# Moving filter-tap sums on GpSimd and the K0 butterfly on VectorE in a Hyena long convolution

## The chip, the cores and the metric

One Trainium2 chip, one core of it. The metric is the device time of the whole program in microseconds, as the median of the runs. The engines are TensorE (PE, with its weight loads as PEld), VectorE (DVE), ScalarE (ACT), GpSimd (POOL) and SyncE (SP), which issues DMAs.

## The reference

The kernel computes one encoder layer for two sequences, a prompt of 1024 tokens and a sample of 512, at a width of 1024: dilated window attention, a bidirectional Hyena branch with two long convolutions one after the other, gates, an output projection and RMS norms. The change lies in the Hyena branch:

```
def _long_conv(z, h_fwd, h_bwd, skip):
    kcirc = jnp.concatenate([h_fwd, jnp.zeros((1, c), jnp.float32), h_bwd[:0:-1]], axis=0)
    spec = jnp.fft.rfft(zf, n=2 * length, axis=1) * jnp.fft.rfft(kcirc, axis=0)[None]
    y = jnp.fft.irfft(spec, n=2 * length, axis=1)[:, :length]
    return y + zf * skip.astype(jnp.float32)
...
    zz = hx1.astype(f32) * _long_conv(hv, filt[:, 0, 0], filt[:, 0, 1], skip[0])
    zz = hx2.astype(f32) * _long_conv(zz, filt[:, 1, 0], filt[:, 1, 1], skip[1])
```

## The kernel before

**Items.** The convolutions run between about 1250 and 2060 us of the span, in 12 items. Items 0 to 7 are long: 256 channels of the prompt at convolution order 0 or 1. Items 8 to 11 are wide: 512 channels of the sample. `wide(i)` tells them apart. Every engine has its own program and passes through the items in order; semaphores hold them together. There are no automatic schedules here; the order on each engine is the order of the code.

**What an item needs.** For each item the filter taps are made on the chip: TensorE makes 8 tiles of taps for forward and backward filters, in four pairs (`gen_pair`, L1263), VectorE multiplies each by its decay (`filt`, L1858, which reads PSUM) into the buffer `hs`, and GpSimd forms the sum and the difference of the forward and backward half of a tile (`sums`, L995 and L996, in `tge`). In long items only tiles 0 to 3 have such sums. The even butterfly (`even_butterfly`, L1893 to L1900, on `tge`) prepares slab K0 of the filter, the odd butterfly (`butterfly_shifted`, L1913 to L1926, on `hs`) the second slab, and the time butterfly (L1893 to L1900 again, on the transposed signal `tz`) the signal's. These are SBUF to SBUF, on VectorE. Two slabs of memory serve for all three in turn, so that a time butterfly overwrites the slab that K0's transforms read and waits for them.

**What a period on VectorE looks like.** `product(i)` goes over four frequency pairs p. For each, it does two filter tiles of the next item (L1858), then the product of signal and filter spectra: two instructions for the real part of the signal (L1964, from PSUM), two for the imaginary part, and one addition in SBUF (L1974). For p = 3, when the next item is long, the even butterfly of the next item comes in front of the filter tiles. Behind the four pairs come the odd and the time butterfly of the next item, then `recombine` twice (L2043 to L2063), which finishes the inverse transform and multiplies with the gate.

**GpSimd beside it.** For each pair it does `sums` of tiles 2p and 2p + 1 of the next item (nothing for tiles above 3 in a long item), then `combine_long`: L1005 adds the two products of the real part, once they are done; L1009 and L1010 add the imaginary parts, once L1974 has run. The event of L1010 (`f_y`) releases the inverse transform of the pair on TensorE and the reuse of the product buffers. A `sums` waits for its filter tile (`f_gen_used`) and, through `f_bf`, for the odd butterfly of the item before.

**TensorE.** `signal_dft` weaves the filter's transforms (K, L1268), the generation of filter pairs (L1263) and the signal's transforms (Z, L1268, one real and one imaginary bank a pair); then the signal of the next item is turned (`to_time`, L1342), inverses 0 and 1 (L1324), the K0 transforms of the next item (L1268, 36 matmuls), which wait for the even butterfly, and inverses 2 and 3. The next item's K transforms wait for the odd butterfly, its Z for the time butterfly. ScalarE copies the results out of PSUM.

**SP.** `load_filter` loads the decay table of the item after (`c_dec`) once the last filter tile of the item in front has been multiplied.

Of the kernel before, what the change touches and what calls it, by code (L numbers as in the profile page):

```python
# [241 lines left out]
def build(nc, ins, cst, y_p, y_s):  # L242
# [7 lines left out]
    with ExitStack() as ctx:  # L250
# [231 lines left out]
        NI = len(ITEMS)  # L482
# [4 lines left out]
        def wide(i):  # L487

            return ITEMS[i][0] == 1

        def chans(i):

            s, q, o = ITEMS[i]
            n = 4 if s else 2
            return n * q, n
# [5 lines left out]
        def zc_of(i):  # L501
            return planes(zc[ITEMS[i][1] % 2], i)
# [16 lines left out]
        def gen_tile(i, j):  # L519

            m, h = j // 2, j % 2
            return (2 * (m % 2) + h, m // 2) if wide(i) else (j, 0)
# [22 lines left out]
        def kernel_units(p):  # L545

            return [K0_UNITS + p, K0_UNITS + 5 + p] + ([K0_UNITS + 4] if p == 0 else [])
# [45 lines left out]
        def wait_free(eng, u):  # L593
            eng.wait_ge(bank_free[u[0]], u[1] + 1)
# [125 lines left out]
        def ot_count(n):  # L720

            return n // 3 + 1
# [16 lines left out]
        def w_allmax(pool, b):  # L739
            pool.wait_ge(S["w_amax"], b + 1)  # L740
            if b >= 3:
                pool.wait_ge(S["w_scale"], b - 2)
            pool.partition_all_reduce(amax_all[b % 3], amax[b % 3], P, bass.bass_isa.ReduceOp.max).then_inc(S["w_all"], 1)  # L743
# [173 lines left out]
        def _(pool):  # L917
# [66 lines left out]
            def sums(i, j):  # L984

                if not wide(i) and j >= 4:
                    return
                t, x = gen_tile(i, j)
                h = hs[:, j % 4 if wide(i) else t, :]
                pool.wait_ge(S["f_gen_used"], GEN0[i] + j + 1)  # L990
                if i >= 1:
                    pool.wait_ge(S["f_bf"], 3 * i - 1)
                c = slice(FQ * x, FQ * x + FQ)
                ge, go = (tge[:, t, c], tgo[:, t, c]) if wide(i) else (tge[:, t, 0:FQ], tge[:, t, FQ:2 * FQ])
                nc.gpsimd.tensor_tensor(ge, h[:, 0:FQ], h[:, FQ:2 * FQ], ALU.add)  # L995
                nc.gpsimd.tensor_tensor(go, h[:, 0:FQ], h[:, FQ:2 * FQ], ALU.subtract).then_inc(S["f_ge"], 1)  # L996

            def combine_long(i, p):

                g = PR0[i] + p  # L1000
                pr, pi = pq[p % 2], pq[2 + p % 2]
                y = yf[:, 2 * p:2 * p + 2, :].rearrange("p b (a c) -> p b a c", a=2)
                part_ = pi[:, 0:4 * FQ].rearrange("p (b a c) -> p b a c", b=2, a=2)
                wait_free(pool, uz[i][2 * p])
                nc.gpsimd.tensor_tensor(yf[:, 2 * p:2 * p + 2, :].rearrange("p b c -> p (b c)"), pr[:, 0:4 * FQ], pr[:, 4 * FQ:8 * FQ],  # L1005
                                        ALU.add).then_inc(S["f_r"], 1)
                pool.wait_ge(S["f_r"], g + 1)
                pool.wait_ge(S["f_im"], g + 1)
                nc.gpsimd.tensor_tensor(y[:, :, 0, :], y[:, :, 0, :], part_[:, :, 1, :], ALU.subtract)  # L1009
                nc.gpsimd.tensor_tensor(y[:, :, 1, :], y[:, :, 1, :], part_[:, :, 0, :], ALU.add).then_inc(S["f_y"], 1)  # L1010

            def combine_wide(i, n):

                a = pq[n % 2]
                if n % 2 == 0:
                    pool.wait_ge(S["f_pq"], 4 * (i - WIDE0) + n // 2 + 1)
                else:
                    wait_free(pool, uz[i][n])
                nc.gpsimd.tensor_tensor(yf[:, n, 0:FQ], a[:, 0:FQ], a[:, 3 * FQ:4 * FQ], ALU.subtract)
                nc.gpsimd.tensor_tensor(yf[:, n, FQ:2 * FQ], a[:, FQ:2 * FQ], a[:, 2 * FQ:3 * FQ], ALU.add  # L1020
                                        ).then_inc(S["f_y"], 1)

            def load_og(t):
                pool.dma_start(ogt[t % 2], og_d[:, P * t:P * t + P, :, :].rearrange("g p a c -> p g a c")).then_inc(ld_og[t % 2], 16)
# [2 lines left out]
                sums(0, j)  # L1027
            for i in range(NI):
                for p in range(4):
                    if i + 1 < NI:  # L1030
                        sums(i + 1, 2 * p)
                        sums(i + 1, 2 * p + 1)
                    if wide(i):
                        combine_wide(i, 2 * p)
                        combine_wide(i, 2 * p + 1)
                    else:
                        combine_long(i, p)
                s, q, o = ITEMS[i]
                if i + 1 == NI:
                    w_allmax(pool, PREPARED)  # L1040
                    w_allmax(pool, PREPARED + 1)
                if o == 1:
                    pool.wait_ge(S["f_post"], 2 * (i + 1))
                    if i + 1 == NI:
                        for sl in range(3):
                            pool.wait_ge(ot_out[sl], 16 * ot_count(6 * NT - 1))
                        load_og(0)
                        load_og(1)
                    c, nch = chans(i)
                    pool.dma_start(hy_d[c:c + nch, :, TOK0[s]:TOK0[s] + LENS[s]].rearrange("c p t -> p c t"),  # L1050
                                   zc_of(i)).then_inc(hy_out[q % 2], 16)
# [654 lines left out]
        def _(dve):  # L1706
# [7 lines left out]
            def settle():  # L1714
                dve.wait_ge(S["dve_steps"], steps[0])
# [167 lines left out]
            def butterfly(i, x, src):  # L1883

                a = butterfly_buffer(i, x)
                w = 2 * FQ
                f = src.rearrange("p t c -> p (t c)")

                def A(c):
                    return a[:, c, :]  # L1890

                lower, upper = (f[:, 2 * w * n:2 * w * n + 2 * w].rearrange("p (a c) -> p a c", a=2) for n in range(2))
                chain(dve.tensor_tensor(a[:, A2R:A2N + 1, :], lower, upper, ALU.subtract))  # L1893
                chain(dve.tensor_tensor(a[:, A0:A4 + 1, :], lower, upper, ALU.add))
                settle()
                e1 = A(A4)
                chain(dve.scalar_tensor_tensor(A(A1R), A(A2N), RT, f[:, 0:w], ALU.mult, ALU.add))
                chain(dve.scalar_tensor_tensor(A(A3R), A(A2N), -RT, f[:, 0:w], ALU.mult, ALU.add))
                chain(dve.scalar_tensor_tensor(A(A1N), e1, RT, f[:, 2 * w:3 * w], ALU.mult, ALU.add))
                dve.scalar_tensor_tensor(A(A3I), e1, -RT, f[:, 2 * w:3 * w], ALU.mult, ALU.add).then_inc(S["f_bf"], 1)  # L1900
# [27 lines left out]
            def even_butterfly(i):  # L1928

                dve.wait_ge(S["f_ge"], SUM0[i + 1])  # L1930
                butterfly(i, 0, tge)

            def odd_butterfly(i):

                if wide(i):
                    butterfly(i, 1, tgo)
                else:
                    butterfly_shifted(i)
# [66 lines left out]
            def product(i):  # L2005
                settle()
                for n in range(1, K0_UNITS):
                    wait_free(dve, uk[i][n])
                for p in range(4):
                    if i + 1 < NI:  # L2010
                        if p == 3 and not wide(i + 1):
                            even_butterfly(i + 1)
                        filt(i + 1, 2 * p)
                        filt(i + 1, 2 * p + 1)
                    if wide(i):
                        wait_free(dve, uk[i][K0_UNITS + p])
                        product_wide(i, 2 * p)
                        product_wide(i, 2 * p + 1)
                    else:
                        for n in kernel_units(p):  # L2020
                            wait_free(dve, uk[i][n])
                        product_long(i, p)
# [47 lines left out]
            for i in range(NI):  # L2070
                product(i)
                if i + 1 < NI:
                    if wide(i + 1):
                        even_butterfly(i + 1)
                    odd_butterfly(i + 1)
                    time_butterfly(i + 1)
                M0 = PREPARED
                if i + 1 == NI:
                    w_max(dve, M0)
                    w_max(dve, M0 + 1)  # L2080
                    w_split(dve, chain, settle, M0)
                made = 3 * min(i + 2, NI)
                recombine(i, 0, made)
                recombine(i, 1, made)
# [189 lines left out]
            for t in range(NT):  # L2274
# [17 lines left out]
                for half in range(2):  # L2292
                    n = MT_O + 2 * t + half
                    for x in range(2):
                        j = 2 * half + x
# [32 lines left out]
```

## Time and profile before

| what | value |
|---|---|
| median of 3 runs | 2871.57 us (2869.19 to 2871.99) |
| profiled execution | 2870.86 us |
| its span | 2869.1 us |
| mean granted TensorE clock | 0.971 |
| busy PE, DVE, ACT, POOL | 2661.8, 1536.3, 845.0, 429.3 us |

The page gives the span, each engine's busy time, the granted clock of TensorE as a share of full speed (2.4 GHz), and the chain that ended last. Over the whole span TensorE is the busiest engine, at 93%. The convolution stage differs: between 1300 and 1770 us VectorE has nine tenths or more in nearly every slice. A timeline row gives start and duration in us, engine, line and operation, with the number of instructions merged in it, and in brackets the idle time in front and what ended it. The start of the next instruction can lie a little in front of the end of the one before.

### The profile page before, as it was taken

To read this page: it belongs to the slowest core of one execution; us is meant where nothing else is said; L and a number is where in the kernel's file an instruction comes from. 1 tells how busy PE (TensorE), PEld (TensorE's weight loads), DVE (VectorE), ACT (ScalarE), POOL (GpSimd) and SP (SyncE) were. 2 spreads that over 40 slices of the span, in tenths; PEclk is the share of its full clock that TensorE was granted. 3 is DMA by queue.
4 is the path that set the end of the run, shared out by engine and by line. 5 is a ranking of instruction groups with operands and counts; after the bars stand their busy time and mean duration, and the time that the engine had idled before them with its cause. 6 is when DMAs were issued, how large, how long until landed. Compare 5 with 4: busy or idle time off the path is not lost. (4 is left out here: it accounts for less than half of the span.)

```text
span 2869.1 us, 34380 instructions
## 1 busy us (share of the span) xinstructions
PE 2661.8 (93%) x13660; PEld 1532.5 (53%) x13660; DVE 1536.3 (54%) x2151; ACT 845.0 (29%) x1707; POOL 429.3 (15%) x515
## 2 busy tenths in 40 slices
PE   5999999999999999969888898699988999999897
PEld 2444444667676766745545554346533444444487
DVE  6354441323232322248999999588785243633443
ACT  5232331334343443532222222112342122311132
POOL 0000000000000000013344444253210000000000
PEclk8999999999999999979999999899999999999999
DMA  5522221101010110030112111211632020100122
GB/s 204 212 88 85 85 89 59 36 27 53 27 53 29 49 45 20 20 127 15 33 48 71 58 37 59 69 42 44 214 124 88 30 103 1 59 30 30 52 75 88
DMA packets 103766, 192.08 MB, mean 67 GB/s; under 512 B 4927, under 2 KB 78887, under 8 KB 103224
## 3 DMA queue, kind: packets, MB, share of 16 engines
q1 hardware_dynamic: 88280, 115.05, 12.6%
q0 software_dynamic: 15184, 68.56, 6.4%
q10 hardware_dynamic: 144, 6.29, 0.7%
q8 instruction: 109, 1.79, 0.3%
q14 instruction: 49, 0.40, 0.0%
HBM read 141.55 MB, written 54.62 MB: 68 GB/s over the span
## 5 line engine op out<-in xcount | busy, mean ns | idle before, releaser
L1101 PE MATMUL ps<-mem 128*128 128x512 f16 (+1 forms) x9312 | 1735.0, 347 | 28.6 <-DVE mem L2265 8.0
L1101 PEld LDWEIGHTS ps<-mem 128*128 128x128 f16 x9312 | 929.6, 102 | 792.6 <-issue 42.0
L1268 PE MATMUL ps<-mem 128*128 128x512 f32 (+1 forms) x1104 | 451.2, 562 | 47.8 <-DVE mem L1926 19.4
L1268 PEld LDWEIGHTS ps<-mem 128*128 128x128 f32 x1104 | 212.6, 197 | 279.1 <-issue 256.9
L1824 DVE TENSOR_TENSOR mem<-ps,mem 128x512 f32<-128x512 f32 (+2 forms) x144 | 79.9, 555 | 436.7 <-PE ps L1202 407.8
L780 DVE SCALAR_TENSOR_TENSOR mem<-mem 128x2048 f16<-128x2048 f32 (+1 forms) x56 | 127.2, 2273 | 125.6 <-ACT mem L755 125.6
L1528 ACT ACTIVATE mem<-ps 128x512 f32<-128x512 f32 (+1 forms) x144 | 72.5, 504 | 410.7 <-PE ps L1215 410.7
L755 ACT ACTIVATE mem<-mem 128x2048 f16<-128x2048 f32 (+1 forms) x56 | 108.6, 1940 | 284.9 <-DVE mem L773 277.0
L1324 PE MATMUL ps<-mem 128*128 128x256 f32 x768 | 169.1, 379 | 0.0
L1324 PEld LDWEIGHTS ps<-mem 128*128 128x128 f32 x768 | 145.1, 190 | 20.1 <-issue 1.0
L1801 DVE SCALAR_TENSOR_TENSOR mem<-mem 128x1537 f32<-128x1537 f32 x24 | 43.7, 1819 | 186.4 <-ACT mem L1474 186.4
L743 POOL PARTITION_ALL_REDUCE mem<-mem x56 | 25.5, 457 | 759.5 <-DVE mem L736 753.4
L1520 ACT ACTIVATE mem<-mem 128x256 f32<-128x256 f32 (+1 forms) x288 | 129.6, 456 | 8.2 <-DVE mem L1830 8.0
L1964 DVE TENSOR_TENSOR mem<-ps,mem 128x1024 f32<-128x1024 f32 x112 | 129.2, 1211 | 1.5 <-PE ps L1268 1.5
L736 DVE TENSOR_REDUCE mem<-mem 128x1 f32<-128x2048 f32 (+1 forms) x56 | 123.2, 2203 | 3.9 <-DMA mem<-in_w_in 3.8
L983 POOL DMA_DIRECT2D s_og<-mem x72 | 39.4, 547 | 563.8 <-ACT mem L1536 563.8
L1677 ACT ACTIVATE mem<-ps,mem 128x512 f32<-128x512 f32 x69 | 46.1, 683 | 245.7 <-PE ps L1101 245.7
L1230 PE MATMUL ps<-mem 128*128 128x64 f32 x896 | 116.6, 268 | 0.0
L1230 PEld LDWEIGHTS ps<-mem 128*128 128x128 f32 x896 | 112.2, 193 | 0.0
L1263 PE MATMUL ps<-mem 64*128 64x512 f32 x192 | 60.6, 711 | 55.5 <-DVE mem L1858 36.9
L1469 ACT ACTIVATE mem<-ps,mem 128x512 f32<-128x512 f32 x72 | 48.8, 685 | 192.5 <-PE ps L1101 192.5
L1858 DVE TENSOR_TENSOR mem<-ps,mem 128x512 f32<-128x512 f32 x96 | 62.6, 679 | 55.3 <-DMA mem<-c_dec 42.7
(180 smaller groups left out, 2312.3 us busy)
## 6 DMA issues: line engine op xcount, KB each, us to landing
mem<-in_w_in SPq DMA_DIRECT2D x44, 1024.0 KB, 5.2
s_uc<-mem POOLq DMA_DIRECT2D x24, 768.5 KB, 3.9
mem<-s_uc SPq DMA_DIRECT2D x18, 1024.0 KB, 6.2
s_og<-mem POOLq DMA_DIRECT2D x72, 132.0 KB, 2.0
mem<-s_og POOLq DMA_DIRECT2D x12, 792.0 KB, 4.9
mem<-c_dec SPq DMA_DIRECT2D x8, 896.0 KB
s_hn<-mem POOLq DMA_DIRECT2D x1, 6912.0 KB, 19.7
mem<-s_hn SPq DMA_DIRECT2D x3, 2304.0 KB, 20.4
```

The lines of the kernel that those rows point to most:

```text
L736: dve.tensor_reduce(amax[b % 3], raw_of(b).rearrange("p k c -> p (k c)"), AX.X, ALU.max, apply_absolute_value=True).then_inc(S["w_amax"], 1)
L755: act.activation(w_place(b)[:, 0, 0:chunks(b)], raw_of(b), ACT.Copy, scale=wscale[b % 3]).then_inc(S["w_hi"], 1)
L780: dve.scalar_tensor_tensor(w[:, 1], raw_of(b), wscale[b % 3], w[:, 0], ALU.mult, ALU.subtract).then_inc(S["w_lo"], 1)
L1101: mm = pe.matmul(out, lhs(a, k), rhs(b, k), start=(k == 0 and x == 0), stop=(k == kc - 1 and x == 2))
L1230: mm = pe.matmul(ps[:, 6 + t % 2, c], pt[N % 2][:, x, P * b:P * b + P], vt[H % 2][:, vi, c], start=(b == 0), stop=(b == len(vs) - 1))
L1268: mm = pe.matmul(out, ftab[:, P * tab:P * tab + P], a[:, comp, :], start=(x == 0), stop=(x == len(terms) - 1))
L1324: mm = pe.matmul(ps[:, fbank(u), FQ * lane + oc:FQ * lane + oc + w], yf[:, 2 * p + b, FQ * im + c:FQ * im + c + P], itab[:, col:col + w], ...
L1520: act.activation(pr[N % 2][:, x, 0:kw], lg[N % 2][:, x, 0:kw], ACT.Exp, bias=o[:, c:c + 1], accum_out=o[:, c + HH:c + HH + 1]).then_inc(S[ ...
L1528: act.activation(pt[N % 2][:, :, 0:kw], ps[:, 4 + N % 2, :].rearrange("p (x c) -> p x c", x=2)[:, :, 0:kw], ACT.Copy).then_inc(S["a_ptcopi ...
L1824: dve.tensor_tensor(l[:, :, c0:c1], ps[:, 2 + N % 2, :].rearrange("p (x c) -> p x c", x=2)[:, :, c0:c1], bias, ALU.add).then_inc(S["a_bias ...
L1858: op = dve.tensor_tensor(h.rearrange("p (e c) -> p e c", e=2), ps[:, n % 2, :].rearrange("p (e c) -> p e c", e=2), d.to_broadcast([P, 2, F ...
L1964: op = dve.tensor_tensor(o.rearrange("p k a c -> p (k a) c"), z.unsqueeze(1).to_broadcast([P, 4, FQ]), k.rearrange("p k a c -> p (k a) c") ...
```

## The change

On GpSimd, when this item and the next are both long, the sums of tiles 0 and 1 stand as before in front of combination 0; those of tile 2 follow combination 1, and those of tile 3 follow combination 2. In all other items the order is as before. On VectorE, the even butterfly of a long next item moves from the front of pair 3 to behind pair 3, where it already stood for a wide next item. No instruction is added or taken out.

```
             for i in range(NI):
                 for p in range(4):
+                    first, later = range(2 * p, 2 * p + 2), range(0)
+                    if not wide(i) and i + 1 < NI and not wide(i + 1):
+                        first, later = range(2 if p == 0 else 0), range(p + 1, p + 2) if p in (1, 2) else range(0)
                     if i + 1 < NI:
-                        sums(i + 1, 2 * p)
-                        sums(i + 1, 2 * p + 1)
+                        for j in first:
+                            sums(i + 1, j)
                     if wide(i):
                         combine_wide(i, 2 * p)
                         combine_wide(i, 2 * p + 1)
                     else:
                         combine_long(i, p)
+                    if i + 1 < NI:
+                        for j in later:
+                            sums(i + 1, j)
...
                 for p in range(4):
                     if i + 1 < NI:
-                        if p == 3 and not wide(i + 1):
-                            even_butterfly(i + 1)
                         filt(i + 1, 2 * p)
                         filt(i + 1, 2 * p + 1)
...
             for i in range(NI):
                 product(i)
                 if i + 1 < NI:
-                    if wide(i + 1):
-                        even_butterfly(i + 1)
+                    even_butterfly(i + 1)
                     odd_butterfly(i + 1)
                     time_butterfly(i + 1)
```

## Rows read from the trace of the kernel before

**Rows 1.** Windows: length, busy us of PE, PEld, DVE, ACT, POOL; clock, DMA.

```profile
1434.22:1501.89 67.67, 58.54 (x200) 34.24 (x200) 66.36 (x79) 15.03 (x31) 28.58 (x20) 1.00 0.12 35
```

**Rows 2.** Waits of VectorE and TensorE, 1366 to 1772 us: total, times, longest.

```profile
DVE mem L2043 <- issue: 1.1, 6, 0.2
...
PE ps L1268 <- DVE mem L1926: 15.5, 6, 2.7
```

**Rows 3.** Timeline of VectorE in one long item: start, us, engine, line, shapes.

```profile
1447.97 2.96 DVE L1974 TENSOR_TENSOR mem<-mem 128x1024 f32<-128x1024 f32 x1
...
1452.04 4.60 DVE L1964 TENSOR_TENSOR mem<-ps,mem 128x1024 f32<-128x1024 f32 x4
1456.75 1.23 DVE L1974 TENSOR_TENSOR mem<-mem 128x1024 f32<-128x1024 f32 x1
1457.89 1.22 DVE L1893 TENSOR_TENSOR mem<-mem 128x1024 f32<-128x1024 f32 x1
...
1464.73 1.28 DVE L1858 TENSOR_TENSOR mem<-ps,mem 128x512 f32<-128x512 f32 x2
...
1484.75 1.23 DVE L1893 TENSOR_TENSOR mem<-mem 128x1024 f32<-128x1024 f32 x1
```

**Rows 4.** Timeline of GpSimd in the same long item.

```profile
1447.50 2.34 POOL L1005 TENSOR_TENSOR mem<-mem 128x1024 f32<-128x1024 f32 x1
...
1454.46 2.36 POOL L1005 TENSOR_TENSOR mem<-mem 128x1024 f32<-128x1024 f32 x1 [0.89 <-DVE mem L1964]
1458.12 2.12 POOL L1009 TENSOR_TENSOR mem<-mem 128x512 f32<-128x512 f32 x1 [1.30 <-DVE mem L1974]
```

**Rows 5.** Durations of single lines, ns min/median/max; last, a group: us, mean ns.

```profile
L1974 DVE TENSOR_TENSOR mem<-mem x32: 1224/1226/2975, 1301.9 to 1803.8; 128x1024 f32<-128x1024 f32 x32
L1894 DVE TENSOR_TENSOR mem<-mem x28: 1211/1220/2300, 1273.8 to 2002.6; 128x1024 f32<-128x1024 f32 x28
L1897 DVE SCALAR_TENSOR_TENSOR mem<-mem x28: 691/692/1649, 1275.0 to 2003.9; 128x512 f32<-128x512 f32 x28
L1914 DVE TENSOR_TENSOR mem<-mem x8: 1221/2292/2293, 1278.7 to 1743.6; 128x1024 f32<-128x1024 f32 x8
L1916 DVE TENSOR_TENSOR mem<-mem x8: 2292/3242/3246, 1280.0 to 1745.9; 128x2048 f32<-128x2048 f32 x8
...
L1974 DVE TENSOR_TENSOR mem<-mem 128x1024 f32<-128x1024 f32 x28 | 44.7, 1596 | 2.9
```

**Rows 6.** Timeline of VectorE and GpSimd in item 7, pair 2.

```profile
1791.03 4.59 DVE L1964 TENSOR_TENSOR mem<-ps,mem 128x1024 f32<-128x1024 f32 x4
1795.72 2.29 DVE L1974 TENSOR_TENSOR mem<-mem 128x1024 f32<-128x1024 f32 x1
...
1794.58 2.35 POOL L1005 TENSOR_TENSOR mem<-mem 128x1024 f32<-128x1024 f32 x1
```

**Rows 7.** Timeline of TensorE, with the idle time in front in brackets.

```profile
1436.21 1.13 PE L1263 MATMUL ps<-mem 64*128 64x512 f32 x4 [2.17 <-DVE mem L1858]
...
1467.18 7.93 PE L1268 MATMUL ps<-mem 128*128 128x256 f32 x36
1474.95 7.07 PE L1324 MATMUL ps<-mem 128*128 128x256 f32 x32
1484.77 5.39 PE L1268 MATMUL ps<-mem 128*128 128x512 f32 x12 [2.75 <-DVE mem L1926]
...
1503.88 1.88 PE L1263 MATMUL ps<-mem 64*128 64x512 f32 x4 [2.17 <-DVE mem L1858]
...
1813.78 10.99 PE L1268 MATMUL ps<-mem 128*128 128x512 f32 x20 [7.46 <-DVE mem L1900]
...
1850.38 2.08 PE L1263 MATMUL ps<-mem 64*128 64x512 f32 x4 [11.83 <-DMA mem<-in_filt_w]
```

**Rows 8.** Windows of TensorE: length, busy us, granted clock, DMA.

```profile
1813.78:1818.10 4.32, 4.32 (x5) 0.50 0.02 4
...
1850.38:1855.70 5.32, 5.32 (x8) 0.50 0.57 175
```

More of the change, by code:

```diff
@@ L1029, in _ @@
                 for p in range(4):
+                    first, later = range(2 * p, 2 * p + 2), range(0)
+                    if not wide(i) and i + 1 < NI and not wide(i + 1):
+                        first, later = range(2 if p == 0 else 0), range(p + 1, p + 2) if p in (1, 2) else range(0)
                     if i + 1 < NI:
-                        sums(i + 1, 2 * p)
-                        sums(i + 1, 2 * p + 1)
+                        for j in first:
+                            sums(i + 1, j)
                     if wide(i):
@@ L1037, in _ @@
                         combine_long(i, p)
+                    if i + 1 < NI:
+                        for j in later:
+                            sums(i + 1, j)
                 s, q, o = ITEMS[i]
@@ L2010, in product @@
                     if i + 1 < NI:
-                        if p == 3 and not wide(i + 1):
-                            even_butterfly(i + 1)
                         filt(i + 1, 2 * p)
@@ L2072, in _ @@
                 if i + 1 < NI:
-                    if wide(i + 1):
-                        even_butterfly(i + 1)
+                    even_butterfly(i + 1)
                     odd_butterfly(i + 1)
```

## The prediction

> **What bounds the kernel now.** I first read the windows of busy time over one long item, which is the stretch that the change touches. A long item repeats every 67.67 us, VectorE is busy for 66.36 us of it, TensorE for 58.54 us and GpSimd for 28.58 us [rows 1]. The next view, the waits, shows the same from the other side: in the six periods from 1366 to 1772 us VectorE waited for 1.1 us in all, and not once for another engine, while TensorE stood 15.5 us behind the odd butterfly (L1926) alone [rows 2]. So in long items VectorE's instructions, laid end to end, are the time, and a microsecond taken out of them is a microsecond of the kernel, until TensorE becomes late.
>
> The next question is whether VectorE's instructions are as short as they could be. The timeline of one period answers it. L1974 adds two 1024-wide tensors that both lie in SBUF; it takes 2.96 us for pair 1 and 1.23 us for pair 2 [rows 3]. GpSimd's timeline shows why: its L1005 ran from 1447.50 to 1449.84, across the start of L1974 at 1447.97, and L1974 ended at 1450.93, which is 1.09 us after L1005's end. For pair 2, L1005 ended at 1456.82 and L1974 began at 1456.75: an overlap of 0.07 us, no price [rows 3, 4]. It works in the other direction too: L1009 starts 0.23 us after L1893, and takes 2.12 us, as though it had stood behind it [rows 4]. I read this as turns: an instruction of VectorE with two SBUF inputs and one of GpSimd don't run at once, each waits for the other's whole instruction. The products L1964, which read one input from PSUM, run beside GpSimd at full speed.
>
> The page of durations gives the prices. The shortest of a line is its clean time, the longest the contended one: L1974 1.224 and 2.96 (six of 28 are long: the 28 sum to 44.7 us, clean they would be 34.3, and the excess of 10.4 is six times 1.73); L1894 1.22 and 2.30; L1897 0.69 and 1.65; L1914 1.22 and 2.29; L1916 2.29 and 3.25 [rows 5].
>
> **The change, part by part**, for the seven items i = 0 to 6, where this item and the next are long. Nothing moves for i = 7 and the wide items, since there the code takes its old branch.
>
> *Sums 2 and 3 behind the combinations.* No GpSimd instruction is added or removed. In front of combination 1, GpSimd now runs sums 2 and 3 (four instructions at a pitch of 0.69, 2.76 us), which is why L1005 starts at 1447.50 instead of right behind the real half of product 1. That half ends at about 1445.6, as product 2's half, begun at 1452.04, is followed by L1005 2.42 us later, at 1454.46 [rows 3, 4]. After the change L1005 of pair 1 starts at about 1445.67, ends at 1448.0, and L1974 of pair 1 costs 1.23: a gain of 1.74. Then GpSimd does L1009, L1010 to 1451.8, sum 2 to 1453.15, and only then L1005 of pair 2. With product 2 begun at 1450.3 its natural start is 1452.7: it is 0.44 late. The price of a late L1005 can be read in item 7, where more sums lie in front: product begun at 1791.03, L1005 at 1794.58, so 1.13 later than the natural 2.42, and L1974 takes 2.29, 1.06 more [rows 6]. So lateness is paid nearly in full, less 0.07. I take 0.37 for pair 2 and, with the same arithmetic (sum 3 ends at 1460.55, natural start 1460.1), 0.36 for pair 3. Bounds of this pair of prices: nothing at all, and 2 x 1.73 if each were as late as L1005 of pair 1 is now.
>
> *Even (K0) butterfly behind the last products.* Today it starts right behind L1974 of pair 2, just as GpSimd has L1009 and L1010 to do, and L1894 and L1897 pay 1.08 + 0.96 = 2.04 [rows 3, 5]. Its place is taken by filters 6 and 7 and product 3, which read PSUM, so they pay nothing. Product 3 must find its inputs ready without the 6.84 us of cover that the butterfly gave: TensorE's bank of the real part of pair 3 is free when product 2's half is read, at 1452.7, and four matmuls take 1.8 us; the imaginary part is done near 1456.9. Product 3 reads at 1457.7 and 1460.0. So no wait. At the end the even butterfly, not the odd one, stands behind the last L1974, and takes over the meeting with L1009 and L1010: it pays 2.04 again, and the odd butterfly is freed of 1.07 + 0.96 = 2.03 [rows 5].
>
> Sum for one period: 1.74 + 2.04 - 2.04 + 2.03 - 0.37 - 0.36 = 3.04 us, a period of 64.6. Item 0 is different: there VectorE waits for TensorE, L1974 of pair 1 is clean already (six long ones for items 1 to 6), so it gains 2.03 less about 0.35, 1.7 us. In all 6 x 3.04 + 1.7 = 19.9 us.
>
> *What TensorE does with the later even butterfly.* Its program has to_time, inverses 0 and 1, K0 transforms, inverses 2 and 3, then the next item's transforms. Today K0 (7.93 us) starts at 1467.18, long after the even butterfly's end at 1464.7, the inverses follow at 1474.95 and TensorE then stands 2.75 us [rows 7]. After the change the even butterfly ends at about 1470.75 while TensorE is through with inverse 1 at about 1465.7: a new stop of 5.1 us, behind which everything on TensorE's queue waits. The 2.75 us of stop before the next item's transforms is then gone, and TensorE begins them at about 1485.7, 4.0 us after the odd butterfly. Who waits for that? VectorE's time butterfly overwrites the slab that K0 reads: K0 is done at 1478.7, the time butterfly wants it at 1481.7. The recombination wants the last inverse at 1486.8; it is copied at 1484.7. The next item's product 1 wants Z1. Going round this loop: K0 7.8, inverses 7.1, transforms 16.9 (1484.77 to the idle before 1503.88), filter pair 1.1, Z1 1.8 to 2, and VectorE from product 1 to the even butterfly's end 27.5: 62.3, with a few hand-overs 62.6 [rows 3, 7]. Against 64.6 that leaves 2.0 us. VectorE stays the bound, narrowly.
>
> The stop also meets the clock. After a stop of 7.46 us the granted clock was 0.50 (1.2 GHz) for the 4.32 us that followed, and the 20 matmuls took 10.99 us, where 12 take 5.39 at 2.4 GHz, so 2.0 us were lost [rows 7, 8]. A stop of 5.1 us I take to cost 1.7 to 2.6 us of K0, just the slack. I charge 0.3 us a period for it: 19.9 - 1.8 = 18 us. Ends: nothing, and 1.4 us a period (twice such a loss, 3.4 us against 2.0).
>
> The Trainium skill has a rule that speaks against this part: "TensorE: Matmul & The Clock Gate", section "Why this matters for your kernels", advises against idle gaps between matmul bursts, since the clock falls back to half. By that rule K0 would run slow in each item; the rows agree that the clock falls after a stop, and it is rival 3 that says what it would take to lose by it.
>
> **DMAs.** load_filter waits for the last filter of an item, which now comes about 7 us sooner, so the decay table is loaded sooner and lands sooner. The stores of item results hang on recombination, and move along with it. Nothing on SP's or GpSimd's queue is passed.
>
> **After the long items** all is released by events, so the shift of item 7 reaches the end. The profiled execution took 2870.86 (span 2869.1), 0.7 less than the median of 2871.57. From the profiled execution: 2870.86 - 18 = 2852.9; on the scale of the median 2853.6.
>
> **Rivals.** 1: *the forecast*, turns are avoided, VectorE stays the bound, 0.72. Own range 2848 to 2858.
>
> 2: *TensorE takes over.* The clock's loss is 3.4 us in each period and the loop comes to 66.0. The gain is 1.66 x 6 + 1.7 = 11.7, so 2860. For it: the slack is only 2.0. Against: after 7.46 us of stop the loss was no more than 2.0. Chance 0.13.
>
> 3: *slower.* The late even butterfly leaves TensorE at 1.2 GHz for most of K0 and the inverses. It decides from (67.67 - 62.6) x 2 = 10.1 us at half clock in each period. After a stop of 11.83 us the low clock still covered the next 5.32 us of matmuls [rows 8]. If 14 us of each period's matmuls ran at half clock, a loss of 7 us, the loop would be 69.6, and the whole 1.9 x 6 = 11 us slower less item 0's 1.7: 2881. Chance 0.05.
>
> 4: *nothing is gained, the meetings only move.* GpSimd's backlog makes L1005 late by a full 1.73 at pairs 2 and 3: 3.77 - 3.46 = 0.3 us a period, 2869. Or the long instructions have another cause than GpSimd. The Trainium skill, "Advanced Engine Details and Errata", section "VectorE Performance Modes", names only instructions in a two-port mode as blocked by GpSimd; by it these plain fp32 additions would pay nothing, and moving them would leave 2871.6. Here rows 3 to 6 go the other way, since the 1.09 us behind L1005's end recurs in item 7 (1796.93 to 1798.01). Chance 0.10.
>
> **How the numbers follow.** Likeliest 2853.6. Rival 2 and the unknown cost of the clock carry the range up to 2862; down, no clock loss (2851.7), and lateness that costs nothing (0.73 x 6 + 0.35 more, 4.7) give 2847. Chances, with 0.2% (5.7 us) as what can be told from no change: faster 0.85 (forecast and rival 2), same 0.10, slower 0.05.
>
> **What the profile would show.** Right: long periods of 64.6 to 65; L1974 of pair 1 at 1.23 and of pairs 2 and 3 near 1.6; L1894 and L1897 long once an item still, L1914 and L1916 clean at 1.22 and 2.29; a TensorE stop near 5 us on L1900 in front of K0, and the waits on L1926 gone. Wrong: VectorE waiting on TensorE at L2043 or L1964 (rival 2), a granted clock of 0.50 over 10 us of a period (rival 3), L1974 of pairs 2 and 3 near 2.9 (rival 4).

## The result, and the profile after

The changed kernel takes 2856.19 us as the median of 4 runs (2854.04 to 2858.79), the kernel before 2871.78 us in its 4. The ratio is 0.9947, with a 95% interval from 0.9932 to 0.9962: 15.6 us, 0.5%. The profiled execution took 2854.04 us, its span is 2852.0, which is 17.1 us below the span of before.

Line numbers on TensorE's and VectorE's side have moved by six: L1858, L1893, L1894, L1897, L1900 are L1864, L1899, L1900, L1903 and L1906 in the changed kernel; L1914, L1916, L1926 are L1920, L1922, L1932; L1964 and L1974 are L1970 and L1980; L1268 and L1324 are L1274 and L1330. L2043 has moved by four, to L2047. GpSimd's L995 to L1010 stay.

The first view is that of [rows 1], the window of one long item:

```profile
1430.52:1495.36 64.84, 59.56 (x201) 35.41 (x200) 63.17 (x79) 15.23 (x31) 26.75 (x20) 0.97 0.12 37
```

The period is 64.84 us where it was 67.67. It is the same to 0.03 us in all six. VectorE's busy time fell by 3.19 us, though its 79 instructions are the same ones. The timeline of VectorE in that period, against [rows 3]:

```profile
1444.26 1.22 DVE L1980 TENSOR_TENSOR mem<-mem 128x1024 f32<-128x1024 f32 x1
...
1446.91 4.62 DVE L1970 TENSOR_TENSOR mem<-ps,mem 128x1024 f32<-128x1024 f32 x4 [0.22 <-PE ps L1274]
1451.63 1.27 DVE L1980 TENSOR_TENSOR mem<-mem 128x1024 f32<-128x1024 f32 x1
...
1458.72 1.63 DVE L1980 TENSOR_TENSOR mem<-mem 128x1024 f32<-128x1024 f32 x1
1460.27 1.21 DVE L1899 TENSOR_TENSOR mem<-mem 128x1024 f32<-128x1024 f32 x1
1461.41 2.28 DVE L1900 TENSOR_TENSOR mem<-mem 128x1024 f32<-128x1024 f32 x1
...
1466.48 0.68 DVE L1906 SCALAR_TENSOR_TENSOR mem<-mem 128x512 f32<-128x512 f32 x1
1467.30 1.23 DVE L1919 TENSOR_TENSOR mem<-mem 128x1024 f32<-128x1024 f32 x1
```

L1980 of pair 1 is down from 2.96 to 1.22. That of pair 3 is up to 1.63. The even butterfly now stands behind it and is the one that pays (L1900 at 2.28). GpSimd's timeline, against [rows 4], shows L1005 on time for pair 1 (1441.97, and its end at 1444.33 is just past the start of L1980) and late for pair 3 (product 3 began at 1454.02, the natural start is 1456.44):

```profile
1441.97 2.36 POOL L1005 TENSOR_TENSOR mem<-mem 128x1024 f32<-128x1024 f32 x1 [0.89 <-DVE mem L1970]
...
1449.45 2.37 POOL L1005 TENSOR_TENSOR mem<-mem 128x1024 f32<-128x1024 f32 x1
...
1456.90 2.37 POOL L1005 TENSOR_TENSOR mem<-mem 128x1024 f32<-128x1024 f32 x1
1460.49 2.11 POOL L1009 TENSOR_TENSOR mem<-mem 128x512 f32<-128x512 f32 x1 [1.23 <-DVE mem L1980]
```

The durations, against [rows 5]. The odd butterfly (L1920, L1922) never meets GpSimd now, since its longest is as short as its shortest:

```profile
L1920 DVE TENSOR_TENSOR mem<-mem x8: 1216/1218/1219, 1279.3 to 1727.8; 128x1024 f32<-128x1024 f32 x8
L1922 DVE TENSOR_TENSOR mem<-mem x8: 2291/2292/2294, 1280.6 to 1729.1; 128x2048 f32<-128x2048 f32 x8
...
L1980 DVE TENSOR_TENSOR mem<-mem 128x1024 f32<-128x1024 f32 x28 | 37.2, 1330 | 2.9
```

The waits of VectorE and TensorE over the six periods, against [rows 2]:

```profile
DVE mem L1970 <- PE ps L1274: 1.4, 6, 0.3
DVE mem L2047 <- issue: 1.1, 6, 0.2
...
PE ps L1274 <- DVE mem L1906: 30.4, 6, 5.1
```

The wait for the odd butterfly is gone, and one for the even butterfly has come, six times 5.1 us. And VectorE waits for TensorE once a period, 0.22 to 0.26 us in front of product 2, which it never did before. TensorE's timeline, against [rows 7]:

```profile
1455.14 7.07 PE L1330 MATMUL ps<-mem 128*128 128x256 f32 x32
1467.31 9.53 PE L1274 MATMUL ps<-mem 128*128 128x256 f32 x36 [5.09 <-DVE mem L1906]
1476.68 7.07 PE L1330 MATMUL ps<-mem 128*128 128x256 f32 x32
```

And TensorE's windows behind the stop, with the granted clock as the third figure, against [rows 8]:

```profile
1467.31:1470.50 3.19, 3.19 (x8) 0.52 0.03 8
1470.50:1476.68 6.18, 6.18 (x31) 1.00 0.00 0
```

K0 takes 9.53 us where it took 7.93: about 3.1 us at its start ran at half clock (1.2 GHz; the 0.52 of the first window is a mean), and half of that is the 1.6 us by which it grew.

### The profile page after: what moved, and what is told of

Read it like the earlier page. It is cut to its first block and busy times, and to the rows that moved or that the text cites. A ratio compares the mean times of both kernels' runs of the same rounds, so it can differ in the third digit from the quotient of the medians.

```text
span 2852.0 us, 34380 instructions
## 1 busy us (share of the span) xinstructions
PE 2659.1 (93%) x13660; PEld 1537.8 (54%) x13660; DVE 1515.5 (53%) x2151; ACT 846.2 (30%) x1707; POOL 416.3 (15%) x515
## 5 line engine op out<-in xcount | busy, mean ns | idle before, releaser
L1274 PE MATMUL ps<-mem 128*128 128x512 f32 (+1 forms) x1104 | 449.1, 562 | 49.5 <-DVE mem L1906 45.6
L1274 PEld LDWEIGHTS ps<-mem 128*128 128x128 f32 x1104 | 215.9, 200 | 273.9 <-issue 254.6
L1330 PE MATMUL ps<-mem 128*128 128x256 f32 x768 | 169.1, 379 | 0.0
L1330 PEld LDWEIGHTS ps<-mem 128*128 128x128 f32 x768 | 145.1, 190 | 20.1 <-issue 1.0
L1970 DVE TENSOR_TENSOR mem<-ps,mem 128x1024 f32<-128x1024 f32 x112 | 129.2, 1210 | 3.0 <-PE ps L1274 3.0
L1864 DVE TENSOR_TENSOR mem<-ps,mem 128x512 f32<-128x512 f32 x96 | 62.5, 678 | 55.8 <-DMA mem<-c_dec 43.2
```

The source lines that it names most:

```text
L1274: mm = pe.matmul(out, ftab[:, P * tab:P * tab + P], a[:, comp, :], start=(x == 0), stop=(x == len(terms) - 1))
L1330: mm = pe.matmul(ps[:, fbank(u), FQ * lane + oc:FQ * lane + oc + w], yf[:, 2 * p + b, FQ * im + c:FQ * im + c + P], itab[:, col:col + w], ...
L1864: op = dve.tensor_tensor(h.rearrange("p (e c) -> p e c", e=2), ps[:, n % 2, :].rearrange("p (e c) -> p e c", e=2), d.to_broadcast([P, 2, F ...
L1970: op = dve.tensor_tensor(o.rearrange("p k a c -> p (k a) c"), z.unsqueeze(1).to_broadcast([P, 4, FQ]), k.rearrange("p k a c -> p (k a) c") ...
```

## The experiments

The main theory: instructions of VectorE with two SBUF inputs and those of GpSimd take turns, and VectorE's sum is the period. A meeting is short for one such instruction that has to stand behind one of the other engine. The rivals: TensorE's loop, with the clock behind the new stop, is what sets it; or GpSimd has nothing to do with the long instructions. Periods are read from the start of `filt`'s first tile (L1858 of before) in one item to that in the next, as in the windows above. Each run has line numbers of its own, that of its kernel.py.

**e1: GpSimd's half alone.** Against the changed kernel:

```diff
                     if i + 1 < NI:
+                        if p == 3 and not wide(i + 1):
+                            even_butterfly(i + 1)
                         filt(i + 1, 2 * p)
...
-                    even_butterfly(i + 1)
+                    if wide(i + 1):
+                        even_butterfly(i + 1)
```

> The GpSimd half of the change alone: sums 2 and 3 behind combinations 1 and 2, the even butterfly still in front of pair 3. Theory (turns between GpSimd and VectorE instructions with two SBUF inputs, VectorE bound): L1974 of pair 1 falls from 2.96 to 1.23 us, but the even butterfly now waits for sum 3, which ends 3.9 us after L1974 of pair 2; in return it meets no GpSimd instruction (2.04 less). Period 67.66 - 1.74 + 0.37 + 3.95 - 2.04 = 68.2 us, in all about 5 us slower than before: 2877 us. Rival (the long L1974 was all that mattered): 6 x 1.73 = 10 us faster, 2861.

It took 2878.5 us (ratio 1.0024, interval 1.0015 to 1.0033), 7.6 us slower than before, with a period of 68.40. VectorE's waits over six periods:

```profile
DVE mem L1899 <- POOL mem L996: 24.3, 6, 4.0
```

And its timeline from L1980 of pair 2 on:

```profile
1459.79 1.59 DVE L1980 TENSOR_TENSOR mem<-mem 128x1024 f32<-128x1024 f32 x1
1465.42 1.22 DVE L1899 TENSOR_TENSOR mem<-mem 128x1024 f32<-128x1024 f32 x1 [4.04 <-POOL mem L996]
1466.56 1.22 DVE L1900 TENSOR_TENSOR mem<-mem 128x1024 f32<-128x1024 f32 x1
```

The even butterfly stands 4.04 us behind sum 3, as expected, and is clean in return. L1980 of pair 2, 1.59 us here, shows the price of the late L1005 (0.36 us, where 0.37 was worked out) without TensorE's wait beside it. The rival that sees only the long L1974 is out. This half by itself loses.

**e2: VectorE's half alone.** The order of GpSimd is that of before, the even butterfly stands behind product 3:

```diff
-                    first, later = range(2 * p, 2 * p + 2), range(0)
-                    if not wide(i) and i + 1 < NI and not wide(i + 1):
-                        first, later = range(2 if p == 0 else 0), range(p + 1, p + 2) if p in (1, 2) else range(0)
                     if i + 1 < NI:
-                        for j in first:
-                            sums(i + 1, j)
+                        sums(i + 1, 2 * p)
+                        sums(i + 1, 2 * p + 1)
...
-                    if i + 1 < NI:
-                        for j in later:
-                            sums(i + 1, j)
```

> The VectorE half alone: the even butterfly behind product 3, sums 2 and 3 still in front of combination 1. Theory: L1974 of pair 1 stays at 2.96, pairs 2 and 3 are clean at 1.23, the odd butterfly is clean (2.03 less), one hand-over of 0.19 more: VectorE's own period 65.8 us, TensorE's loop about 66.1. In all 10 + 1.8 = about 12 us faster than before: 2860 us. Rival (the late K0 costs TensorE what VectorE gains): near 2870.

It took 2861.14 us (0.9963, 0.9951 to 0.9976), 9.8 us faster. The period is 65.85 us in four of six cases and 66.4 in two. So VectorE's half alone wins nearly two thirds of what the whole change wins. The halves don't add: 9.8 less 7.6 is 2.2 us, and together they give 15.6. e1 loses by VectorE's wait for sum 3, and the later even butterfly takes that wait away. The two longer periods are the first sign of the clock: in them VectorE waited up to 0.7 us at recombination for ScalarE's copy of the last inverse, and K0 took 10.7 and 10.6 us, where it took 9.4 to 9.7 in the other four.

**e3: the sums of tiles 2 and 3 left out**, but for 8 columns of the difference, so that this part of the filter is not computed, to see who sets the period once GpSimd is never late:

```diff
-                nc.gpsimd.tensor_tensor(ge, h[:, 0:FQ], h[:, FQ:2 * FQ], ALU.add)
-                nc.gpsimd.tensor_tensor(go, h[:, 0:FQ], h[:, FQ:2 * FQ], ALU.subtract).then_inc(S["f_ge"], 1)
+                w = 8 if not wide(i) and j >= 2 else FQ
+                if w == FQ:
+                    nc.gpsimd.tensor_tensor(ge, h[:, 0:FQ], h[:, FQ:2 * FQ], ALU.add)
+                nc.gpsimd.tensor_tensor(go[:, 0:w], h[:, 0:w], h[:, FQ:FQ + w], ALU.subtract).then_inc(S["f_ge"], 1)
```

> The changed kernel with the sums of tiles 2 and 3 left out but for 8 columns of the difference (that part of the filter is not computed). Theory A, TensorE's loop sets the period now: L1005 is on time, L1974 of pair 3 is 1.23 instead of 1.62, and the wait in front of product 2 stays: period 64.84 - 0.39 - 0.04 = 64.4 us. Theory B, VectorE's instructions alone set it and the wait is an accident: the wait goes as well, 64.1 us.

In a single run it took 2852.82 us. All additions of the imaginary part (L1974 of before) in items 0 to 6 are at 1.23, so nothing is late on GpSimd, and yet the periods are 64.69 to 65.15, and only the one of 64.69 is shorter than in the changed kernel. Both expectations missed. VectorE's wait in front of product 2 grew, up to 0.8 us, and TensorE's K0 is longer although the stop in front of it is shorter. TensorE's timeline, in two periods:

```profile
1533.00 9.70 PE L1276 MATMUL ps<-mem 128*128 128x256 f32 x36 [4.65 <-DVE mem L1908]
...
1597.58 10.19 PE L1276 MATMUL ps<-mem 128*128 128x256 f32 x36 [4.65 <-DVE mem L1908]
```

So theory A was right that TensorE's loop now counts, but took K0 as fixed. It isn't. The one short period, 64.69, begins after the K0 of 9.70 at 1533.00; the others begin after K0s of 10.1 to 10.6 and take 64.96 to 65.15. The stop in front of K0 is 4.65 us in all of them. So K0's time at half clock makes the difference between these periods, and the length of the stop doesn't.

**e4: a fill in the stop.** The changed kernel with matmuls that nothing reads:

```diff
+            def fill_stop(i):
+                u = uk[i + 1][0]
+                wait_reuse(pe, u)
+                for _ in range(10 if not wide(i + 1) else 0):
+                    pe.matmul(ps[:, fbank(u), :], ftab[:, 0:P], ftab[:, 0:2 * FQ], start=True, stop=True)
...
                 if i + 1 < NI and not wide(i):
+                    fill_stop(i)
                     filter_dft(i + 1, range(K0_UNITS))
```

> The changed kernel with 10 matmuls of 128x512 (about 4.5 us) that nothing reads in TensorE's stop of 5.1 us in front of K0; they write the bank that K0's first transform overwrites. If the half clock at K0 sets the period: K0 takes 7.9 instead of 9.5 us, the wait in front of product 2 goes, period 64.5. If VectorE's turns take over at once: the wait of 0.25 goes, but L1974 of pair 2 pays for its late L1005 (1.6 instead of 1.26), period stays within 0.1 of 64.84.

In a single run it took 2863.24 us, with a period of 66.58. The fill was sized wrongly: one matmul of fp32 shows as two instructions in the trace, and I had taken 0.45 us for a matmul where it is that of one instruction. TensorE's timeline, the fill and K0:

```profile
1464.96 8.75 PE L1356 MATMUL ps<-mem 128*128 128x512 f32 x20
1473.54 7.93 PE L1274 MATMUL ps<-mem 128*128 128x256 f32 x36
```

8.75 us went into a stop of 5.1, so TensorE was simply full. Two things can be read all the same: K0 is back at 7.93 us once nothing stops in front of it, and TensorE's own work is 66.58 - 8.6 - 0.2 = 57.8 us a period (8.6 is the fill from start to start of the next group).

**e5: VectorE does the last imaginary combination itself**, a direct test of the price of a meeting:

```diff
+                if p == 3:
+                    return
                 pool.wait_ge(S["f_r"], g + 1)
...
+                if p == 3:
+                    dve.wait_ge(S["f_im"], g + 1)
+                    dve.wait_ge(S["f_r"], g + 1)
+                    chain(dve.tensor_tensor(y[:, :, 0, :], y[:, :, 0, :], part_[:, :, 1, :], ALU.subtract))
+                    dve.tensor_tensor(y[:, :, 1, :], y[:, :, 1, :], part_[:, :, 0, :], ALU.add).then_inc(S["f_y"], 1)
```

> The changed kernel, but VectorE itself does the two 512-wide additions of the imaginary part of combination 3 (L1009 and L1010 of GpSimd), right behind L1974 of pair 3. Theory (turns): the even butterfly meets nothing, 2.03 less a period, and the two instructions cost 2 x 0.60 plus about 0.15 of hand-over: period 64.84 - 0.7 = 64.15 us; with item 7 about 5.5 us faster than the changed kernel: 2850.5. Rival (it is not a matter of turns, GpSimd's help is worth its 2.5 us): 1.2 us a period slower, 2865.

It took 2850.67 us (0.9931, 0.9918 to 0.9945) against 2870.34 of before in the same comparison. VectorE's timeline behind the addition of pair 3, the two new instructions and the start of the even butterfly:

```profile
1457.95 0.69 DVE L1988 TENSOR_TENSOR mem<-mem 128x512 f32<-128x512 f32 x1
1458.56 0.68 DVE L1989 TENSOR_TENSOR mem<-mem 128x512 f32<-128x512 f32 x1
1459.16 1.22 DVE L1901 TENSOR_TENSOR mem<-mem 128x1024 f32<-128x1024 f32 x1
1460.30 1.22 DVE L1902 TENSOR_TENSOR mem<-mem 128x1024 f32<-128x1024 f32 x1
```

Two additions that VectorE makes in 1.2 us cost it 2.0 when GpSimd makes them while VectorE works in SBUF. The butterfly is clean. The periods, though, are 64.37 to 65.04 where 64.15 was expected.

**e6: the four instructions of sums 2 and 3 spread one by one over GpSimd's gaps.** In this cut, which leaves out the body of `sums`, a third argument of `sums` names the half of a tile's sums to do (0 the sum, 1 the difference).

```diff
-                        first, later = range(2 if p == 0 else 0), range(p + 1, p + 2) if p in (1, 2) else range(0)
+                        first, later = range(2 if p == 0 else 0), [((2, 0),), ((2, 1), (3, 0)), ((3, 1),), ()][p]
...
-                        for j in later:
-                            sums(i + 1, j)
+                        for j, half in later:
+                            sums(i + 1, j, (half,))
```

> The changed kernel, with the four instructions of sums 2 and 3 spread one by one: one behind combination 0, two behind 1, one behind 2. Theory: L1005 of pair 3 is on time, L1974 of pair 3 falls from 1.62 to 1.23 us, all else stays: period 64.45 us, 2.7 us in all, 2853.5. If TensorE's loop alone sets the period and doesn't contain pair 3: 64.84 as now.

2851.44 us (0.9933, 0.9919 to 0.9946). All additions of the imaginary part in items 0 to 6 are at 1.23; the first four periods are 64.6, near the 64.45 expected, the last two 64.97.

**e7: e5 and e6 together**, the case that separates the theories: VectorE has 1.2 us less to do than in the changed kernel.

> The two before this together. Theory: the gains add, since both lie in VectorE's part of the loop (product 1 to the end of the even butterfly) and in VectorE's own sum: period 63.75 us, about 8.5 us under the changed kernel, 2847.5. If TensorE stops this at its own pace: 64.4 or more, 2853.

2851.72 us (0.9933, 0.9919 to 0.9946), no faster than either part. The periods are 64.86 to 65.05. Waits of VectorE over six of them:

```profile
DVE mem L1974 <- PE ps L1278: 4.5, 6, 0.8
DVE mem L2058 <- ACT mem L1609: 4.3, 6, 0.7
DVE mem L1903 <- DVE mem L1936: 1.1, 5, 0.3
```

TensorE's timeline at K0:

```profile
1532.38 10.71 PE L1278 MATMUL ps<-mem 128*128 128x256 f32 x36 [3.97 <-DVE mem L1910]
```

And TensorE's windows, the first from within the stop:

```profile
1531.30:1538.10 6.80, 5.72 (x14) 0.52 0.00 0
1538.10:1542.90 4.80, 4.80 (x24) 1.00 0.00 0
```

The stop (1528.4 to 1532.38) is down to 3.97 us, the half clock covers its last 1.35 us, and about 5.5 of K0's 10.71 us ran at it instead of 3.1 of 9.53. VectorE waits about 1.7 us a period, 1.5 of it at product 2 and at recombination, for work that stands behind K0 on TensorE.

**e8: e7 with 8 such matmuls**, with the same mistake in the fill's size as in e4:

> As the one before, with 8 matmuls (3.6 us) in TensorE's stop in front of K0, so that K0 runs at full clock. If the half clock at K0 is what is left: 0.3 us a period less than the one before, 63.4. If VectorE is the bound: the same within 0.1 us, L1974 of pair 2 near 1.6 and no wait in front of product 2.

2851.3 us (0.993, 0.9917 to 0.9942), period 64.86. K0 took 7.93, but the fill took 6.9 us instead of 3.6, and 57.8 + 6.9 + 0.2 of short waits is the period: TensorE was full. It tells nothing on VectorE, and agrees with the 57.8 of e4.

**e9: the changed kernel with a fill of the right size**, 5 matmuls.

> As e4, with the fill sized from e4's own trace: there 10 matmuls took 8.75 us, more than the stop of 5.1, so now 5, about 4.4 us. Theory (VectorE's turns and TensorE's loop lie level in the changed kernel): K0 takes 7.9 instead of 9.5 us, the wait of 0.25 in front of product 2 goes, L1974 of pair 2 pays 1.6 instead of 1.26 for its late L1005: period within 0.1 of 64.84, time within 1 us of the changed kernel's 2856. Rival (the half clock is what holds it): 64.5 or less, 2853.

2854.21 us (0.9938, 0.9922 to 0.9954). The periods are 64.84 to 64.89. K0 takes 8.0 us, VectorE waits for no other engine, and L1974 of pair 2 went from 1.26 to 1.58. TensorE's row of K0, and VectorE's of the addition of pair 2 (L1974 of before, here L1988):

```profile
1468.23 8.01 PE L1274 MATMUL ps<-mem 128*128 128x256 f32 x36 [1.12 <-DVE mem L1914]
...
1452.23 1.58 DVE L1988 TENSOR_TENSOR mem<-mem 128x1024 f32<-128x1024 f32 x1
```

In the period the theory is met to the tenth: take the half clock away, and GpSimd's turns take over at the same length. The time is 2.0 us under the changed kernel's where 1 was allowed, and lies between the theory's and the rival's; with runs that spread by 3 to 5 us it can't decide, the periods do.

**e10: e7 with 5 such matmuls.**

> e7 with 5 such matmuls (4.4 us) in the stop. In e7 VectorE waits 0.75 us at product 2, 0.72 at recombination and 0.24 at the time butterfly in each period, all for TensorE, whose K0 takes 10.7 us there. If that is the half clock: K0 7.9 us, the three waits go, period 64.9 - 1.7 = 63.2 to 63.6, about 9 us under e7, 2842.5. If TensorE is bound by its own work (57.8 us a period by e8's trace, 62.2 with the fill): the same, since that is less than 63.2. Rival (the waits have another cause): 64.9, 2852.

2844.27 us (0.9907, 0.9893 to 0.9921), against 2871.35 of before: 27.1 us faster, and 7.4 under e7, which was measured against a before of 2870.34. All six periods are 63.77 to 63.80. The window of one:

```profile
1429.29:1493.07 63.78, 62.64 (x211) 36.14 (x211) 62.30 (x80) 15.23 (x30) 23.05 (x19) 1.00 0.12 37
```

VectorE's waits over six periods:

```profile
DVE mem L2066 <- issue: 1.1, 6, 0.2
```

And TensorE's timeline, the fill and K0:

```profile
1459.52 4.45 PE L1360 MATMUL ps<-mem 128*128 128x512 f32 x10
1464.01 8.01 PE L1278 MATMUL ps<-mem 128*128 128x256 f32 x36
```

The clock is 1.00 over the whole period, VectorE waits for nobody and TensorE is busy for 62.64 of 63.78 us, 4.4 of them with the fill. Matmuls whose result nothing reads made the kernel 7 us faster. The period is 0.2 us over the range expected, since L1974 of pair 2 pays 1.58 again; that term was left out.

**e11: e7 with 3 such matmuls.**

> As e10 with 3 matmuls (2.6 us), a rest of stop of 2 us or more in front of K0. If a short stop keeps the clock: the same as e10, 63.2 to 63.6. If any stop brings half the clock back for some of K0: K0 9.5 us or more in several periods, period between 63.6 and 64.9.

2844.53 us (0.9905, 0.9891 to 0.9919), periods of 63.78, a stop of 1.8 us in front of K0, and no half clock from the start of item 0's products to that of item 7's. TensorE's row of K0:

```profile
1462.04 8.01 PE L1278 MATMUL ps<-mem 128*128 128x256 f32 x36 [1.75 <-DVE mem L1918]
```

So a rest of stop of this size kept the clock here, and e10 and e11 are equal. Both beat the changed kernel by 12 us.

## Why the prediction was right, point by point

**VectorE's turns with GpSimd: right.** L1974 of pair 1 gave 1.74 (2.96 to 1.22). The meeting moved from the even butterfly in front of pair 3 and the odd one behind it to a single one: the odd butterfly, from L1913 to the time butterfly, fell from 12.97 to 10.94 us, 2.03 as worked out. e1 and e2 give each half its own sign, e5 the price of a meeting from the other side. Item 7, where GpSimd keeps its old order, is the control: there the additions of pairs 1 to 3 still take 2.97, 2.29 and 2.98 us in the changed kernel. Why the two engines take turns is not shown; what is shown is that each waits for the other's whole instruction.

**The late L1005: right in size, in part not paid.** Pair 3 paid 0.40 (0.36 forecast). Pair 2 would have paid 0.36, as e1 and e9 show, but VectorE waited 0.25 us for TensorE there, in which GpSimd caught up; it paid 0.04. Together 0.29, so the two don't add.

**A term was left out.** Behind the even butterfly stood filter tiles, which need nothing of it; now the odd butterfly follows, which starts only when VectorE's earlier steps have ended (`settle`). From the start of L1906 to the next instruction it is 0.82 us instead of 0.60: 0.2 us a period.

**The sum for a period.** 1.74 + 2.03 - 0.31 (from filter 4 to product 2 it is 1.50 us instead of 1.19, the wait among it) - 0.04 - 0.40 - 0.20 = 2.82, and measured 67.66 - 64.84 = 2.82. The prediction had 3.04 less 0.3 for the clock, 2.74. Item 0 gained 71.41 - 69.96 = 1.45 (1.7 forecast, less the same hand-over). In all 6 x 2.82 + 1.45 = 18.4 us from item 0 to item 7, where 18 was forecast. The span shows 17.1, since item 0 began 0.57 us later in this execution, and the part from item 7's start on took 0.7 us more. The median moved by 15.6; the runs of the changed kernel spread over 4.8 us, so the last 2 us can't be told apart. That 2.74 and 2.82 agree so well is in part luck. The unpaid lateness of pair 2 (0.33 us less to pay) covered the hand-over that was left out (0.2), and the 0.3 charged for the clock came out as the longer way from filter 4 to product 2 (0.31).

**"VectorE stays the bound, narrowly": half right.** TensorE's loop was said to have 2.0 us of slack and the clock to cost K0 1.7 to 2.6. It cost 1.6, and yet VectorE waited 0.25 us. The sum for the loop was too small: it closed at product 1, but VectorE's wait is in front of product 2, and that way round is longer. In the changed kernel TensorE works without a stop for 28.2 us from the start of K's transforms (1418.73) to the end of the wait (1446.91), VectorE then needs 20.4 to K0's start (1467.31), and K0 with the inverses behind it takes 16.3 (to 1483.59). At full clock K0 takes 1.6 less and the loop is 63.3 us, not 62.6, so the slack against 64.6 was 1.3 us, less than the 1.6 that the clock took. e9 shows the two to be level: without the half clock the period is 64.87, with it 64.84. So rival 2, TensorE taking over, was nearer than its 0.13 suggested; it came true in e3, e5 and e7. Its price, a fixed loss of 3.4 us, was the wrong form: K0 lost 1.5 us to 3.1 us, and at one length of stop (4.65 us, e2) as little as 1.5 and as much as 2.9.

**Rival 3 (slower by the clock)** had no share: the half clock covered 3.1 us of matmuls a period, not 10. **Rival 4 (the meetings only move)** is refuted by L1974 of pairs 2 and 3 at 1.27 and 1.63 instead of 2.9. The sentence of the Trainium skill on which its second half hung, in "Advanced Engine Details and Errata", section "VectorE Performance Modes", names only two-port modes. The Trainium skill's "GPSIMD Engine Reference", section "1. Specifications", names contention with VectorE instructions with two SBUF inputs too. e1, e2 and e5 agree with that one: the second instruction of the even butterfly takes 1.22 us in e1 and e5, where it meets nothing, and 2.28 in the changed kernel.

## What to carry to other kernels

When VectorE sets the time and GpSimd works beside it, look at the timeline for instructions of one shape with two durations: put GpSimd's work beside VectorE instructions that read PSUM, and let VectorE make a short addition itself if GpSimd would make it while VectorE works in SBUF. After a bottleneck engine has been relieved, read the next engine's stop and its clock together, since a stop in front of matmuls can go on costing behind its end: here stops of 4 to 5.1 us made the 7.9 us of K0 1.5 to 3.1 us longer. And count a matmul's time from groups whose number of matmuls is known, since here fp32 shows two instructions for each (5 matmuls are the x10 of e10).

## What the runs showed of the hardware that was not expected

What a stop cost in clock did not follow from its length. In the long items K0 took 9.5 us behind a stop of 5.1 us (the changed kernel), 9.4 to 10.8 behind 4.65 (e2, e3 and e6), 9.7 to 10.5 behind 4.35 (most periods of e5), 10.7 to 11.1 behind 3.97 (e7), and 7.9 to 8.0 again behind 1.8 us or less. Two periods of e2, with the same stop to 0.01 us:

```profile
1471.95 9.47 PE L1268 MATMUL ps<-mem 128*128 128x256 f32 x36 [4.66 <-DVE mem L1900]
...
1537.80 10.66 PE L1268 MATMUL ps<-mem 128*128 128x256 f32 x36 [4.65 <-DVE mem L1900]
```

In the changed kernel the half clock covers the last 0.3 us of the stop and 3.1 us of K0, in e7 the last 1.35 us of the stop and 5.5 us of K0: both parts are longer there, so it isn't that what left the stop moved onto the matmuls. What decides between a short and a long stretch at half clock is open. e3, e5, e6 and e7 take 0.4 to 1.2 us out of VectorE's work and mostly end between 64.4 and 65.2 us a period. In e7, in e3 and in the last two periods of e6, K0's longer time at half clock holds them there. e10 and e11 show it for e7, since its periods fall from 64.86 or more to 63.78 once K0 is back at 8.0 us; in the others it is inferred from K0's rows. The Trainium skill advises to avoid idle gaps between bursts of matmuls ("TensorE: Matmul & The Clock Gate", section "Why this matters for your kernels"). That holds here with a price of 7 us in the whole kernel: 2851.7 us for e7 and 2844.3 for e10.
